# Split matmuls that read their moving operand and write their bank from the last column to the first

## The reference

```python
proj = h @ w_in[l]
...
x = x + mixed @ w_o[l]
h = rms_norm(x, mlp_norm[l])
x = x + jnp.square(jax.nn.relu(h @ w_up[l])) @ w_down[l]
```

## Time and profile before

| | us |
|---|---|
| runs (3), median | 3117.68 |
| lowest, highest | 3112.34, 3120.33 |
| span of the profiled execution (the page has no time beside it) | 3119.2 |
| PE busy | 3099.6 (99%), 16368 matmuls |
| PE weight loads busy | 2659.7 (85%) |
| VectorE, ScalarE, GpSimd busy | 1839.2, 1465.8, 719.0 |

### The profile page before, as it was taken

How to read it: one execution, slowest core, us unless ns; L and a number is a source line. 1 busy time by engine, 2 the same in 40 slices (tenths; PEclk the granted TensorE clock), 3 DMA queues, 4 the chain that set the end, 5 groups by cost and what they waited for, 6 DMA issues and landing times.

```text
span 3119.2 us, 45296 instructions
## 1 busy us (share of the span) xinstructions
PE 3099.6 (99%) x16368; PEld 2659.7 (85%) x16368; DVE 1839.2 (59%) x2369; ACT 1465.8 (47%) x2274; POOL 719.0 (23%) x746
## 2 busy tenths in 40 slices
PE   8999999999999999999999999999999999999999
PEld 7888888888888888888888888889888888888887
DVE  5676655555555567665555555567686555555554
ACT  5454544444345545454453444552565434444443
POOL 1422241231411143042314150115030101001010
PEclk9999999999999999999999999999999999999999
DMA  6534565655655554455556465657433555555554
GB/s 241 189 142 164 189 219 189 219 189 188 219 189 211 192 187 152 164 182 213 192 188 219 185 219 189 224 213 275 171 120 142 189 199 189 195 192 188 189 188 162
DMA packets 66640, 598.04 MB, mean 192 GB/s; under 512 B 14320, under 2 KB 24816, under 8 KB 31424
## 3 DMA queue, kind: packets, MB, share of 16 engines
q1 hardware_dynamic: 54912, 588.17, 51.7%
q10 hardware_dynamic: 11184, 5.49, 0.7%
q0 software_dynamic: 400, 2.44, 0.2%
HBM read 577.93 MB, written 18.15 MB: 191 GB/s over the span
## 4 chain that ended last, share of the span: by engine, by line
PE 95%; DVE 2%; DMA 1%; ACT 1%; issue 1%; ACTq 0%; DVEq 0%
PE bank L671 93%; DMA urow<-us 1%; PE bank L783 1%; DVE w_lo L1723 1%; PE bank L942 0%; ACT w_hi L1209 0%; PE bank L831 0%; DVE sb L2243 0%; DMA par<-params 0%; DMA u<-urow 0%; DVE w_lo L1717 0%; DVE gbuf L2208 0%; DVE ks L2186 0%; ACT act_hi L1559 0%; DVE act_lo L2216 0%
## 5 line engine op out<-in xcount | busy, mean ns | idle before, releaser
L671 PE MATMUL bank<-xg,w_hi 128*128 128x512 f32 (+1 forms) x4256 | 1434.4, 385 | 1.7 <-issue 1.7
L671 PE MATMUL bank<-xg,w_lo 128*128 128x256 f32 (+1 forms) x4064 | 1142.8, 281 | 0.0
L671 PEld LDWEIGHTS bank<-xg,w_hi 128*128 128x128 f32 x4256 | 789.6, 188 | 168.4 <-issue 2.3
L1717 DVE TENSOR_TENSOR w_lo<-raw,w_hi 128x1024 fp32r<-128x1024 f32 x512 | 668.1, 1341 | 439.4 <-ACT w_hi L1220 439.1
L1220 ACT ACTIVATE w_hi<-raw 128x1024 fp32r<-128x1024 f32 x512 | 514.0, 1052 | 634.4 <-PE bank L671 634.4
L671 PEld LDWEIGHTS bank<-xg,w_lo 128*128 128x128 f32 x4064 | 765.4, 188 | 0.9
L671 PE MATMUL bank<-w_hi,act_hi 128*128 128x512 f32 x1920 | 752.5, 392 | 0.2 <-issue 0.2
L671 PE MATMUL bank<-w_hi,act_lo 128*128 128x512 f32 x1920 | 747.7, 389 | 0.0
L671 PE MATMUL bank<-w_lo,act_hi 128*128 128x512 f32 x1920 | 747.2, 389 | 0.0
L1723 DVE TENSOR_TENSOR w_lo<-raw,w_hi 128x1024 fp32r<-128x1024 f32 x510 | 626.0, 1234 | 170.4 <-ACT w_hi L1209 169.4
L1209 ACT ACTIVATE w_hi<-raw 128x1024 fp32r<-128x1024 f32 x514 | 514.4, 1052 | 174.8 <-PE bank L671 147.6
(11 more groups left out here) (346 smaller groups left out, 2014.9 us busy)
## 6 DMA issues: line engine op xcount, KB each, us to landing
raw<-stream SPq DMA_DIRECT2D x260, 2048.0 KB, 7.7
stabs<-ssm_tabs SPq DMA_DIRECT2D x8, 1176.0 KB, 9.7
rdo<-stabs SPq DMA_DIRECT2D x8, 768.0 KB, 7.3
ssm_bc<-smat SPq DMA_DIRECT2D x8, 640.0 KB, 11.7
raw<-stream SPq DMA_DIRECT2D x4, 1024.0 KB, 8.6
stabs<-ssm_f SPq DMA_DIRECT2D x8, 512.0 KB, 10.8
drv<-stabs SPq DMA_DIRECT2D x8, 512.0 KB, 5.6
trig<-stabs SPq DMA_DIRECT2D x8, 408.0 KB, 5.9
```

Source lines behind the costliest of these rows:

```text
L671: return pe.matmul(o, a, b, start=start, stop=stop, skip_group_check=True)
L1717: dve.tensor_tensor(flat_lo[j][:, 1024 * h:1024 * h + 1024], flat_raw[r][:, 2048 * j + 1024 * h:2048 * j + 1024 * h + 1024], flat_hi[j][:, ...
```

## The change

Every moving operand of the functions named above is read from its last column to its first, and the bank's columns are written from the last to the first, so that each column's result lands where it did before. The stationary operands, the number of matmuls, their order, the waits and all other engines' programs are as before. In `paired_row` the two planes stay in their order and each is reversed by itself.

```diff
             def row_with_meta(b, j, k):
-                mm(bank[b][:, 0:L2], hi[j][:, k, :], xg[:, 0, k, :], k == 0, False)
-                mm(bank[b][:, 0:L2], hi[j][:, k, :], xg[:, 1, k, :], False, False)
-                return mm(bank[b][:, 0:L2], lo[j][:, k, :], xg[:, 0, k, :], False, k == KT - 1)
+                o = bank[b][:, L2 - 1::-1]
+                mm(o, hi[j][:, k, :], xg[:, 0, k, ::-1], k == 0, False)
+                mm(o, hi[j][:, k, :], xg[:, 1, k, ::-1], False, False)
+                return mm(o, lo[j][:, k, :], xg[:, 0, k, ::-1], False, k == KT - 1)
 
             def paired_row(b, j, k):
-                o = bank[b][:, 0:2 * S].rearrange("p (e n) -> p e n", e=2)
-                mm(o, hi[j][:, k, :], xg[:, :, k, META:], k == 0, False)
-                return mm(bank[b][:, 0:S], lo[j][:, k, :], xg[:, 0, k, META:], False, k == KT - 1)
+                o = bank[b][:, 0:2 * S].rearrange("p (e n) -> p e n", e=2)[:, :, ::-1]
+                mm(o, hi[j][:, k, :], xg[:, :, k, :META - 1:-1], k == 0, False)
+                return mm(bank[b][:, S - 1::-1], lo[j][:, k, :], xg[:, 0, k, :META - 1:-1], False, k == KT - 1)
...
             def wide(T, c, t, k0, before=None):
...
-                        o = bank[2 * (c % 2) + m][:]
+                        o = bank[2 * (c % 2) + m][:, ::-1]
                         a_hi, a_lo = (v[:, k, P * m:P * m + P] for v in (act_hi, act_lo))
-                        mm(o, a_hi, wide_hi[t % 2][:, i, :], t == 0 and i == 0, False)
-                        mm(o, a_hi, wide_lo[t % 2][:, i, :], False, False)
-                        last = mm(o, a_lo, wide_hi[t % 2][:, i, :], False, t == 3 and i == 3)
+                        mm(o, a_hi, wide_hi[t % 2][:, i, ::-1], t == 0 and i == 0, False)
+                        mm(o, a_hi, wide_lo[t % 2][:, i, ::-1], False, False)
+                        last = mm(o, a_lo, wide_hi[t % 2][:, i, ::-1], False, t == 3 and i == 3)
```

More of the change, by code:

```diff
@@ L705, in last_wide @@
                         k = (k0 + 12 + i) % KT
-                        o = bank[2 * (c % 2) + m][:]
+                        o = bank[2 * (c % 2) + m][:, ::-1]
                         a_hi, a_lo = (v[:, k, P * m:P * m + P] for v in (act_hi, act_lo))
-                        mm(o, a_hi, wide_hi[1][:, i, :], False, False)
-                        mm(o, a_hi, wide_lo[1][:, i, :], False, False)
-                        last = mm(o, a_lo, wide_hi[1][:, i, :], False, i == 3)
+                        mm(o, a_hi, wide_hi[1][:, i, ::-1], False, False)
+                        mm(o, a_hi, wide_lo[1][:, i, ::-1], False, False)
+                        last = mm(o, a_lo, wide_hi[1][:, i, ::-1], False, i == 3)
                     last.then_inc(tile_done, 1)
@@ L736, in row @@
                     x_hi, x_lo = (xg[:, e, k, META + P * m:META + P * m + P] for e in range(2))
-                    mm(bank[m][:], x_hi, wide_hi[t % 2][:, i, :], k == 0, False)
-                    mm(bank[m][:], x_hi, wide_lo[t % 2][:, i, :], False, False)
-                    return mm(bank[m][:], x_lo, wide_hi[t % 2][:, i, :], False, k == KT - 1)
+                    o = bank[m][:, ::-1]
+                    mm(o, x_hi, wide_hi[t % 2][:, i, ::-1], k == 0, False)
+                    mm(o, x_hi, wide_lo[t % 2][:, i, ::-1], False, False)
+                    return mm(o, x_lo, wide_hi[t % 2][:, i, ::-1], False, k == KT - 1)
                 pe.wait_ge(lo_ready, lo_count(T, 0))
@@ L757, in row @@
                     k = k0 + 4 * t + i
-                    o = bank[b + m][:]
+                    o = bank[b + m][:, ::-1]
                     a_hi, a_lo = (v[:, k, P * m:P * m + P] for v in (act_hi, act_lo))
-                    mm(o, a_hi, wide_hi[t][:, i, :], t == 0 and i == 0, False)
-                    mm(o, a_hi, wide_lo[t][:, i, :], False, False)
-                    return mm(o, a_lo, wide_hi[t][:, i, :], False, t == 1 and i == 3)
+                    mm(o, a_hi, wide_hi[t][:, i, ::-1], t == 0 and i == 0, False)
+                    mm(o, a_hi, wide_lo[t][:, i, ::-1], False, False)
+                    return mm(o, a_lo, wide_hi[t][:, i, ::-1], False, t == 1 and i == 3)
                 pe.wait_ge(lo_ready, lo_count(T, h))
```

## The result

The changed kernel takes 3172.72 us (median of 4 runs, 3165.98 to 3173.89) against 3117.77, a ratio of 1.0175 with a 95% interval of 1.016 to 1.019: **slower** by 1.75%, 12.7 us above the top of the stated range. The profiled execution took 3173.89 us with a span of 3172.1, so 52.9 us of span came on top.

What follows compares the result with a forecast made beforehand. TensorE was taken to bound the kernel, busy 3099.6 of 3119.2 us. All parts summed to 0, giving 3119.2 us by the profiled execution, forecast as 3118 us because the runs' median is 1.5 us less; range 3098 to 3160 us.

Steps and rivals of the forecast that it cites:

- What bounds the kernel: TensorE, busy 3099.6 of 3119.2 us; any matmul cost goes one for one into the end.
- Part 1, the descending read: All touched matmuls: reading the moving operand downwards costs 0, bounded by 2615 us above and −201 us below.
- Part 5, the weight loads: Loads of the stationary operand, which is not reversed, lie beside the matmuls: 0.
- a fixed part: Time per touched matmul beyond one column per cycle: 13.4 ns in `wide`, 13.9 ns an instruction, 201 us in all.
- the price of a jump: In `paired_row`, the read's jump between two runs: 229.4 ns against 226.7 for one run, 2.7 ns.
- part 3: Where the two runs of `paired_row` meet: the write's new jump is covered by the read's, 0; uncovered 10.5 us.
- Parts 2, 3 and 4: Writing the bank downwards, the write's jump in `paired_row`, and issuing the instructions: 0 each.
- The half rate: Rival: descending streams take two cycles per column in every touched matmul, 2615 us more, 5734 us; chance 0.20.
- The small fixed price: Rival: write's jump uncovered in `paired_row`, 3130 us, or every touched matmul starts 2.7 ns late, 3158 us; chance 0.12.
- The jump did not vanish: Rival denied here: descending patterns remove the 2.7 ns at the run's end in `paired_row`, 3109 us; chance 0.08.
- the patterns weren't brought back to ascending ones: Rival denied here: an instruction builder normalises the reversed patterns to ascending, time unchanged; perhaps 0.05.
- What would show it: Signs in start distances: unchanged if right; same few ns in 512s and 272s, fixed price; ratio 512 to 272, rate.

Runs made afterwards that it cites:

- read_only: The changed kernel with moving operands still read descending but banks written ascending, output mirrored; 3167.88 us, 1.0152.
- act_48: The unchanged ascending kernel with six small arrays placed ahead of act_hi, so the stationary tiles of `wide` lie 48 words higher; 3133.5 us, 1.0045.
- the five kernels after it: The unchanged ascending kernel with `par` or `rstd` placed between the two pairs of weight tiles; 3156.19, 3151.07, 3134.25, 3155.44 and 3159.22 us.
- narrow: The unchanged kernel with `wide` keeping only 64 or 32 of 128 stationary columns, two of its four blocks also reading and writing descending; 3143.08 us.
- wide_mix: The unchanged kernel with each of the four blocks of `wide` in its own column order, on both sides; 3127.02 us.
- c=3: Block of `wide` with its two halves of 256 columns swapped, ascending inside, against the unchanged kernel; 226.7 ns between starts.
- write_only: The changed kernel with moving operands read ascending and banks still written descending, output mirrored; 3118.7 us, 0.9996.
- c=2: Block of `wide` with groups of 4 words ascending and words descending inside, against the unchanged kernel; 226.7 ns between starts.
- dense_80: The unchanged kernel with feed-forward activations in rows of 256 instead of 272 words, starting at shift 80 for every k; 3119.48 us, 1.0003.
- asc_twin: The unchanged ascending patterns, tiles placed so reads start in the same 16-byte groups as the change's descending reads; 3174.05 us, 1.0168.

## Why the prediction was wrong, point by point

- *What bounds the kernel* held. TensorE is the end, and nothing absorbed the price.
- *Part 1, the descending read*, is **the step that failed**. It was priced at 0, with one further cycle per column as the only price above. It cost 6.5 ns a matmul in `wide` and 4.2 ns a pair: all of the loss, as `read_only` shows (181.85 us for one iteration, as in the change). The fault lay in the bounds: with a row at one cycle and a row at two, I took the price to be nothing or everything, and left no room for a stall of 16 cycles in 512 columns.
- *Part 5, the weight loads*: "They lie beside the matmuls" was read from busy times. The earlier trace rows shows that they are hidden in time, not that they are free. Of the tiles that the matmuls of `wide` use, `act_48` moves the stationary one alone, and costs 14 us; the five kernels after it move tiles too, and cost 14 to 40 us. The change loses nothing by it, as it leaves the stationary operand where it was; whether its price arises between the two reads was not shown. The Trainium skill, TensorE: Matmul & The Clock Gate, Part 2 (What happens when you issue a matmul), says that loading the next tile's weights does not steal SBUF read bandwidth from the running matmul, as the two have ports of their own. The 226.7 ns that became 229.3, 227.2 and 230.2 in `act_48`, by a move of the stationary tile, show that the running matmul isn't untouched by where that tile lies. That bandwidth is taken from it isn't shown: in `narrow` shorter loads made no matmul faster.
- The warning was in the trace. 226.7 and 229.4 ns for the same 512 columns were written off as a fixed part and as the price of a jump, and the distances that repeat every 8 k were not looked at one by one. The means are 230.8 and 118.4 ns for the two matmuls of a pair, not the 229.4 and 119.4 of part 3. A jump alone needn't cost anything: `wide_mix` c=3 jumps at column 256 on both sides and stays at 226.7.
- *Parts 2, 3 and 4*, the descending write, its jump, and issue, were right at 0: `write_only` 0.9996. By the Trainium skill, PSUM — Partial Sum Buffer, Specifications (TRN2), the descending write should have slowed the matmuls if it counts as non-contiguous; this case's runs show that it does not. The same skill's Advanced Engine Details and Errata, Memory Cachelines, asks for two hits per line; reversed words inside a line (c=2) are free, in agreement, but descending groups of 4 to 16 words, which hit every line as often, pay in full (233.3 ns), and the rule does not show that.
- *The rivals.* The half rate did not occur. The small fixed price came nearest, with the right sign: its upper form, 2.7 ns on all 14,464 instructions, gave 3158 us, and the mean was 3.7 ns. But it named a wrong place (the write's jump or a late start) and a wrong form, as the 272s paid nothing. The jump did not vanish, and the patterns weren't brought back to ascending ones: the reversed read alone has the whole price.
- *What would show it*: the reading "same few ns in 512s and 272s, or in their ratio" knew only two outcomes; the profile showed a third, 6.6 and −0.8 ns.

**What stays open.** Shown: the price is on the reading side; it fell on the matmuls of 512 and 256 columns at one column per cycle, not on the 272s, nor on the fp32 ones at two cycles; the order of words inside 16 bytes is free, that of groups of 16 to 128 bytes is not; ascending matmuls in `wide` change by up to 8.6 ns with placement alone, descending ones hardly at all. That two reading streams get into each other's way at certain addresses would fit much of this and the 226.7 ns of the one lucky placement, but it was only argued: `narrow` and `dense_80` contradict its simplest forms. What the matmuls leave behind for the next ones, and why the 272s pay nothing, isn't known. The order of groups was tried at one placement only.

## What to carry to other kernels

When TensorE is full and its moving operand streams at one column per cycle, compare the distances between starts with columns over clock before saying that anything beside it is free; the 13 ns over in 226.7 had no cause that anyone had measured. An edit of access patterns or of SBUF placement is then worth a measurement even where it moves no byte more: here moving tiles by small arrays and a few words cost up to 1.7% (`asc_twin`), as much as the reversed read. And a kernel that is compared with a change may owe its time to a lucky placement: compare at more than one. Writing the bank in reverse, words reversed within 16 bytes, and reversed reads in matmuls at two cycles per column were free here.

## What the runs showed of the hardware that was not expected

- The same ascending 512-column fp32r matmul takes 226.7 to 235.3 ns from start to start in `wide`, by nothing but where the tiles lie. At shifts 16 and 80 the same three values appear (229.3, 227.2, 230.2), and 32 and 96, 48 and 112 agree in their means, a hint of a period of 64 words.
- Descending reads in `wide` take 233.1 to 234.2 ns at all six placements; at the placement of the kernel before, descending groups of 4, 8 and 16 words take 233.3 to 233.4, of 32 words 232.3, of 128 or 256 words 226.7.
- With all tiles in the same place, the same k of `paired_row` takes 228 ns in one stage and 226 in another: what ran before counts.
- A bank written backwards costs 0.9996 (0.9986 to 1.0005) of one written forwards.
